# Eight projection units opened side by side in a two-block transformer kernel

## The reference, cut to what matters

```python
cs = jax.nn.silu(c)
mod = cs @ ada_w[i] + ada_b[i]              # c: 1 x 1024, ada_w[i]: 1024 x 3072, for i = 0, 1
shift, scale, gate = jnp.split(mod, 3, axis=-1)
h = x * (1.0 + scale) + shift               # x: 256 x 1024
q, k, v, z = jnp.split(h @ moba_w_in, 4)    # moba_w_in: 1024 x 4096; attention on q, k, v, gated by z
```

## Time and profile before

| | us |
|---|---|
| three runs, median (lowest, highest) | 838.95 (838.51, 839.56) |
| the profiled execution | 838.93 |
| its span, first to last instruction | 837.1 |
| busy: PE, DVE, ACT | 818.4, 615.7, 487.6 |
| unit 4 begins on PE (end of the opening) | 40.45 |
| unit 12 begins | 63.48 |
| unit 20 begins | 86.88 |
| mean DMA rate, 3 to 40 us, 44 to 78 us | 420 GB/s, 390 GB/s |

### The profile page before, as it was taken

One profiled execution on the slowest core, in us unless ns is written; L12 is line 12 of the kernel. 1 busy time (PEld: TensorE's weight loads), 2 busy tenths in 40 slices (PEclk: granted clock), 3 DMA queues, 4 the chain that ended last, 5 costly groups with the idle time before them and its releaser, 6 DMA issues.

```text
span 837.1 us, 17642 instructions
## 1 busy us (share of the span) xinstructions
PE 818.4 (98%) x6596; PEld 764.3 (91%) x6596; DVE 615.7 (74%) x1053; ACT 487.6 (58%) x901; POOL 68.2 (8%) x72
## 2 busy tenths in 40 slices
PE   6999999999999999999999999999999999999997
PEld 3899988999999998989898888999999999999885
DVE  4497876768989766977877779664777996888543
ACT  3444575567689754594665457566556554555444
POOL 1000002400001002214100011000002120000000
PEclk9999999999999999999999999999999999999999
DMA  9999963904552221435643426433455454544531
GB/s 374 388 364 391 369 251 143 350 5 151 168 186 99 102 103 52 156 146 191 213 158 144 152 82 221 152 133 142 180 177 201 167 186 155 197 172 179 201 101 50
DMA packets 22012, 153.85 MB, mean 184 GB/s; under 512 B 2496, under 2 KB 2752, under 8 KB 3904
## 3 DMA queue, kind: packets, MB, share of 16 engines
q1 hardware_dynamic: 20592, 145.69, 47.7%
q0 software_dynamic: 1360, 7.34, 2.3%
HBM read 151.97 MB, written 1.05 MB: 183 GB/s over the span
## 4 chain that ended last, share of the span: by engine, by line
PE 87%; DVE 6%; DMA 3%; ACT 3%; issue 1%; SPq 0%; DVEq 0%
PE ps L402 46%; PE ps L1276 7%; PE ps L505 7%; PE ps L475 4%; PE ps L436 2%; PE ps L445 1%; PE ps L467 1%; DVE w_lo L1969 1%; PE ps L842 1%; DMA raw<-in_moba_first 1%; DMA proj<-in_ada_first 1%; PE ps L579 1%; ACT w_hi L1316 1%; PE ps L602 1%; DMA memkv<-in_ada_first 1%
## 5 line engine op out<-in xcount | busy, mean ns | idle before, releaser
L1969 DVE TENSOR_TENSOR w_lo<-raw,w_hi 128x1024 fp32r<-128x1024 f32 x230 | 285.8, 1248 | 94.6 <-ACT w_hi L1316 93.3
L1316 ACT CAST w_hi<-raw 128x1024 fp32r<-128x1024 f32 (+1 forms) x230 | 239.8, 1050 | 164.8 <-PE ps L402 63.1
L402 PE MATMUL ps<-in_hi,w_hi 128*128 128x256 f32 x1120 | 160.8, 286 | 0.1
L402 PE MATMUL ps<-in_lo,w_hi 128*128 128x256 f32 x1120 | 157.2, 283 | 0.0
L402 PE MATMUL ps<-in_hi,w_lo 128*128 128x256 f32 x1120 | 157.1, 283 | 0.0
L402 PEld LDWEIGHTS ps<-in_hi,w_hi 128*128 128x128 f32 x1120 | 144.3, 191 | 4.5 <-issue 3.3
L402 PEld LDWEIGHTS ps<-in_hi,w_lo 128*128 128x128 f32 x1120 | 144.5, 192 | 0.0
L402 PEld LDWEIGHTS ps<-in_lo,w_hi 128*128 128x128 f32 x1120 | 144.3, 192 | 0.0
L2234 DVE SCALAR_TENSOR_TENSOR proj<-work,params,proj 128x256 f32 (+1 forms) x72 | 35.7, 496 | 8.0 <-ACT proj L1536 1.9
L2046 DVE SCALAR_TENSOR_TENSOR work<-raw,cs,work 128x1024 f32 x24 | 30.8, 1285 | 4.8 <-DVE w_lo L1969 1.6
L1276 PE MATMUL ps<-w_hi,in_hi 128*128 128x512 f32 x88 | 34.2, 389 | 0.0
(11 more groups left out here) (444 smaller groups left out, 1363.3 us busy)
## 6 DMA issues: line engine op xcount, KB each, us to landing
raw<-in_mixed SPq DMA_DIRECT2D x24, 1024.0 KB, 7.0
raw<-in_ffn_up SPq DMA_DIRECT2D x22, 1024.0 KB, 4.8
raw<-in_gdn_in SPq DMA_DIRECT2D x16, 1024.0 KB, 4.8
raw<-in_w_in SPq DMA_DIRECT2D x16, 1024.0 KB, 4.8
raw<-in_merge SPq DMA_DIRECT2D x12, 1024.0 KB, 4.8
raw<-in_ffn_down SPq DMA_DIRECT2D x11, 1024.0 KB, 4.7
raw<-in_branch SPq DMA_DIRECT2D x6, 1024.0 KB, 4.7
raw<-in_moba_out SPq DMA_DIRECT2D x4, 1024.0 KB, 6.7
```

The costliest lines, as they stand in the source:

```text
L402: mm = pe.matmul(half(u if bank is None else bank, 0), w[:, u, k * P:(k + 1) * P], a[:, base + k, :], start=(n == 0 and k == 0), stop=(n = ...
L1316: act.copy(w_hi[:, u, :], src).then_inc(hi_done, 1)
L1969: dve.tensor_tensor(w_lo[:, u, :], src, w_hi[:, u, :].bitcast(F32), ALU.subtract).then_inc(lo_done, 1)
```

## The change

The first eight units are now computed side by side, one feature tile after the other. Their weights come as rows: row k holds feature tile k of all eight units (0.5 MB), two rows to a ring slot, the first slot in two transfers, so that row 0 lands alone. `start_row(k, units)` runs the products of row k, first for units 0 and 4 (which share accumulator bank 0), then, behind `ada_columns`, for the other six; the low and high parts of a row are made by ACT and DVE between the operations of the opening. x comes in three transfers (tiles 0-1, 2-3, 4-7) instead of one. `WARM` goes from 11 idle products to 2, and the two idle products behind the second block go. The modulation blocks have semaphores of their own and no longer count as ring slots. The remaining modulation pieces no longer alternate one to one from the start: twelve ring places hold units 8 to 11 and pieces 0 to 7 (`opened`), then 16 units and 16 pieces alternate. The constants are issued after the eighth transfer of the loop instead of the twelfth; both are behind the fourteenth `mixed` transfer.

The core of the diff:

```diff
-WARM = 11
+WARM = 2
...
-ADA_FIRST = GROUP
-MIXED = ADA_FIRST + 16
-PLAIN = MIXED + 2 * 24
+ROWS = 8
+OPENED = (8, 10, 14, 16)
+MIXED = 20
+PLAIN = MIXED + 2 * 16
...
@@ SP @@
         load_ada(0)
-        for g in range(2):
-            sp.dma_start(raw[:, g, :], io["moba_first"][g]).then_inc(sem(f"slot_in{g}"), 16)
-        sp.dma_start(x_t[:], io["x_t"]).then_inc(sem("x_in"), 16)
+        sp.dma_start(raw[:, 0, 0:half_rows], io["moba_first"][0][:, 0:half_rows]).then_inc(sem("first_row_in"), 16)
+        sp.dma_start(x_t[:, 0:2, :], io["x_t"][:, 0:2, :]).then_inc(sem("x_in"), 16)
         load_ada(1)
-        for g in range(2):
-            landed(g)
-        for p in range(2, KT):
-            load_ada(p)
-            landed(p)
-        for c in range(2):
-            load_free(10 + c, io["mixed"][c])
-            landed(8 + c)
-        for start, stop in ((0, 3), (3, 5)):
+        sp.dma_start(raw[:, 0, half_rows:], io["moba_first"][0][:, half_rows:]).then_inc(sem("slot_in0"), 16)
+        load_ada(2)
+        sp.dma_start(x_t[:, 2:4, :], io["x_t"][:, 2:4, :]).then_inc(sem("x_mid_in"), 16)
+        load_rows(1)
+        load_ada(3)
+        landed(0)
+        load_ada(4)
+        load_rows(2)
+        sp.dma_start(x_t[:, 4:KT, :], io["x_t"][:, 4:KT, :]).then_inc(sem("x_rest_in"), 16)
+        landed(1)
+        load_ada(5)
+        load_ada(6)
+        load_rows(3)
+        load_ada(7)
+        for c in range(6):
+            load(4 + c, io["mixed"][c])
+        for start, stop in ((0, 2), (2, 4)):
...
@@ PE @@
+        def start_row(k, units):
+
+            pe.wait_ge(lo_done, place("moba_in", k) + 1)
             pe.wait_ge(*after("in0_hi", k + 1))
...
-        ada_products(1)
-        warm(2)
-        ada_columns(1)
-        ada_products(2)
-        pe.wait_ge(lo_done, 3)
-        start_tile(0)
-        ada_columns(2)
-        for p in range(3, KT):
-            ada_products(p)
-            start_tile(p - 2)
-            ada_columns(p)
-        start_tile(KT - 2)
-        start_tile(KT - 1)
-        pe.wait_ge(lo_done, 4)
-        unit(3)
-        project("moba_in", None, first_group=1, groups=5)
+        bank_pairs = [(u, u + GROUP) for u in range(GROUP)]
+        for k in range(KT - 1):
+            ada_products(k + 1)
+            start_row(k, bank_pairs[0])
+            ada_columns(k + 1)
+            start_row(k, [u for two in bank_pairs[1:] for u in two]).then_inc(unit_done, 1)
+        for two in bank_pairs:
+            start_row(KT - 1, two).then_inc(sem("first_banks"), 1)
+        pe.sem_inc(unit_done, 1)
+        for n in range(ROWS, 12):
+            pe.wait_ge(lo_done, place("moba_in", n) + 1)
+            pe.wait_ge(taken, GROUP + 2 * (n - ROWS + 1))
+            unit(n % GROUP)
+        project("moba_in", None, first_group=3, groups=3)
...
@@ ACT @@
+        highs_ahead = {0: (1,), 3: (4,)}
+        highs_behind = {1: (2, 3), 3: (5,), 5: (6, 7), 6: (8,)}
+        for k in range(KT - 1):
+            copy_rows(k + 1)
+            for n in highs_ahead.get(k, ()):
+                high("moba_in", n)
+            first_input(k + 1)
+            for n in highs_behind.get(k, ()):
+                high("moba_in", n)
+        for u in range(GROUP):
+            act.wait_ge(sem("first_banks"), u + 1)
+            for n in (u, u + GROUP):
+                act.copy(proj[:, n, :], half(u, n // GROUP)).then_inc(taken, 1)
+            if u == 1:
+                high("moba_in", 9)
+        for n in (10, 11):
+            high("moba_in", n)
+        project("moba_in", plain(proj), first_group=2, groups=4)
...
@@ DVE @@
+        lows_ahead = {0: (0,), 4: (4,)}
+        lows_behind = {1: (1,), 2: (2, 3), 4: (5,), 6: (6, 7), 7: (8,)}
...
+        rest(0, 9)
+        low("moba_in", 9)
+        for k, r in ((1, 11), (2, 12), (3, 13)):
+            rest(k, r)
+        low("moba_in", 10)
+        rest(4, 15)
+        low("moba_in", 11)
+        for k, r in ((5, 17), (6, 18), (7, 19)):
+            rest(k, r)
+        with dve.Fori(0, 4) as i:
```

More of the change, by code:

```diff
@@ L79, in place @@
 def place(name, n):
-    if name == "moba_in" and n < GROUP:
+    if name == "moba_in" and n < ROWS:
         return n
+    if name == "moba_in" and n < 12:
+        return OPENED[n - ROWS]
     if name == "moba_in" and n >= 28:
@@ L148, in _program @@
                 at += n
+    later = {"down_done": "ada_rows", "final_sq": "ada_copied", "final_gained": "ada_columns",
+             "final_sum": "mod_tile", "final_scale": "h0"}
+    for name, first in later.items():
+        shared[name], start[name] = first, KT
     sems = {}
@@ L369, in _ @@
         for c in range(2):
-            load(32 + c, io["mixed"][22 + c])
-        for c in range(2):
-            load(34 + c, io["moba_last"][c])
+            load(26 + c, io["moba_last"][c])
         for name, units in STAGES[1:]:
@@ L675, in ada_columns, with first_out @@
             mm.then_inc(sem("ada_columns"), 1)
-        def start_tile(k):
-            last = k == KT - 1
+        def first_out(u):
+            return half(u % GROUP, u // GROUP)
+        def start_row(k, units):
+            pe.wait_ge(lo_done, place("moba_in", k) + 1)
             pe.wait_ge(*after("in0_hi", k + 1))
-            for u in range(3):
-                pe.matmul(half(u, 0), w_hi[:, u, k * P:(k + 1) * P], in_hi[:, k, :], start=(k == 0), stop=False)
-                pe.matmul(half(u, 0), w_lo[:, u, k * P:(k + 1) * P], in_hi[:, k, :], start=False, stop=False)
+            slot = k % GROUP
+            for u in units:
+                pe.matmul(first_out(u), w_hi[:, slot, u * P:(u + 1) * P], in_hi[:, k, :],
+                          start=(k == 0 and u < GROUP), stop=False)
+                pe.matmul(first_out(u), w_lo[:, slot, u * P:(u + 1) * P], in_hi[:, k, :], start=False, stop=False)
             pe.wait_ge(*after("in0_lo", k + 1))
[L685 to L688, removed]
+            for u in units:
+                mm = pe.matmul(first_out(u), w_hi[:, slot, u * P:(u + 1) * P], in_lo[:, k, :],
+                               start=False, stop=(k == KT - 1 and u >= GROUP))
+            return mm
         pe.wait_ge(sem("cs_wide"), 1)
@@ L1379, in copy_rows, with first_input @@
             act.copy(ada_rows[k % 2], half(4 + k % 2, 0)).then_inc(sem("ada_copied"), 1)
[L1381 to L1386, removed]
+        def first_input(k):
             act.wait_ge(*after("h0", k + 1))
@@ L2008, in _ @@
         dve.memset(rows[:], 0.0)
-        for n in range(GROUP):
-            low("moba_in", n)
         flat_mod = mod[:].rearrange("p a b -> p (a b)")
@@ L2029, in _ @@
             dve.wait_ge(sem("mod_tile"), k + 1)
-            if k == 0:
-                dve.wait_ge(*after("x_in", 16))
+            if k in x_parts:
+                dve.wait_ge(*after(x_parts[k], 16))
             dve.tensor_scalar(first_h[:, k, :], x_t[:, k, :], mod[:, 0, 8 + k:9 + k], mod[:, 0, k:k + 1], ALU.mult, ALU.add
                               ).then_inc(sem("h0"), 1)
+            for n in lows_ahead.get(k, ()):
+                low("moba_in", n)
             dve.wait_ge(*after("in0_hi", k + 1))
```

74 lines of the change are left out of this document (42 added, 32 removed).

## The result

| | before | after |
|---|---|---|
| median of 8 runs each, us | 839.2 (838.46 to 840.26) | 843.02 (841.17 to 844.43) |
| ratio, 95% interval | | 1.0042 [1.0032, 1.0052] |
| profiled execution, us (span) | 838.93 (837.1) | 843.13 (841.0) |
| unit 8 begins on PE, us | 51.96 | 50.45 |
| unit 12 | 63.48 | 65.75 |

The account below looks back on a forecast made before the run. PE was taken to bound the kernel, with ring and DVE a parallel chain: 4.8 us won at unit 8, 3.3 lost to DVE's queue, 0.9 left at unit 20. 838.93 - 0.9 = 838.0 us; range 836.2 to 840.6.

Parts of the forecast that it names:

- the 2.5 us that it had allowed itself: Unit 20 on PE: the prediction called itself wrong altogether if it started more than 2.5 us away from 86.
- Block 1 at 11.2: Opening: the second modulation block lands at 10.6, idle products end at 11.2, then its products start at the low clock.
- I take it that the clock is up by then: Opening, row 0 at about 13.15: PE already runs at 2.4 GHz, with products 0.12 us apart.
- Rival 2: Opening: 2.4 GHz comes T later than 12.7 us, each us costing 0.5; chance 0.12 for T under 5, 0.09 above.
- Unit 8 at 47.2: End of the opening on PE: unit 8 begins at 47.2 instead of 51.96, 4.8 us earlier.
- the two waits before rows 2 and 6: Opening on PE: two waits of about 0.3 us each, for the chain from columns to low parts.
- rival 3: Opening: the two waits of the lows are a full operation each, 2.4 for 0.6 us, net +0.9; chance 0.09.
- Unit 12 at 14.8 us behind unit 8: Behind the opening: PE waits 3.3 us in all for DVE's eight rests and five lows; unit 12 at 62.0.
- Wait of about 1 us at unit 20: PE at unit 20, first behind the constants: its transfer holds PE about 1 us more, leaving 0.9 us gained.
- The ring's own part: Fifth mixed transfer issued at 47.1, landed 4.9 us later; fifth to fifteenth takes 31.6 us, to 83.6; unit 20 at 86.0.
- rival 1: Transfers behind the opening: the ring keeps pace, PE has no wait at unit 20; -1.9 to -2.4 us, some 836.8; chance 0.28.
- The hole in the DMA share near 48 us: Sign: the gap in the transfers, before at 40 to 44 us, moves to about 48 us, DMA share under 0.5.

Follow-up runs that it names:

- before, with two idle products: The kernel before with two idle products instead of eleven ahead of block 1, nothing else changed: median 842.33 us, ratio to before 1.0035.
- narrow rests: The changed kernel with rests 0 to 7 on 32 of their 1024 columns, most of the gate sum left out: median 838.97 us, ratio to before 1.0005.
- Waits filled: The changed kernel with two idle products ahead of unit 10 and five ahead of unit 12: median 840.91 us, ratio to before 1.0026.
- rests last: The changed kernel with units 8 to 27 each sharing a transfer with one modulation piece, the last four pieces in two own transfers: 838.76 us, ratio to before 0.9998.
- first slot whole: The changed kernel with the first ring slot in one transfer of 1 MB instead of two halves: median 844.99 us, ratio to before 1.0057.
- five idle products: The changed kernel with five idle products instead of two ahead of block 1: median 843.32 us, ratio to before 1.0047.

## Why the prediction was wrong, point by point

The mechanism of the ring and of DVE's queue was seen; the error is in the clock, twice, and in the first landing. At unit 20 the prediction had 86.0 and the trace has 90.37, 4.4 us too early and outside the 2.5 us that it had allowed itself:

- **Block 1 at 11.2** ("only 1.75 MB between: 6.28 + 4.3", and the idle products to 11.2): 12.35, and row 0 at 14.21 instead of 13.15, so +1.1. The rate of 2.46 us per MB itself was right for 1 MB blocks ("before, with two idle products" waits for block 1 to 16.13), but it didn't hold for the first half row and the first x piece (0.75 MB in 3.8 us). The size of this term was off.
- **"I take it that the clock is up by then, since PE does the same kinds of work up to 12.7":** this is the step that failed. The rate changed near 18.6: row 0 took 5.5 us (14.21 to 19.71) where row 1 took 3.5 (20.71 to 24.21), so +2.0. The kinds of work were the same up to 12.7 but their amount was not: nine idle products were gone, and PE stood 0.9 us for block 1. "Before, with two idle products" shows that this alone can cost 0.5 to 5 us. How much it costs is in part luck: in three other executions with this opening unit 8 came 1.4 to 1.5 us earlier. Rival 2 had this place, with T = 5.9, to which it gave 841.0 and 0.09 for all T above 5; its price of 0.5 per us counts from 12.7, though the forecast had block 1's products at the low rate anyway. The argument against it, that PE has more to do behind 12.7, says nothing of what comes before.
- **Unit 8 at 47.2:** 50.45, which is the two terms above and 0.2 for the two waits before rows 2 and 6 (0.40 each, 0.3 predicted; rival 3 falls). Still 1.5 us earlier than before.
- **Unit 12 at 14.8 us behind unit 8:** measured 15.3, so +0.5. The waits were 1.05 and 2.33 (3.3 in all predicted, 3.38 measured), ended by DVE's lows, and each moved PE by 0.15 more than its own length. From low 9 to low 12 DVE took 13.56 us (50.84 to 64.40), 13.3 predicted. This step was right in place and size; "narrow rests" shows its cause by taking the rests away, and finds 0.8 us there that the ring would have taken anyway.
- **Not in the forecast at all:** a wait of 2.33 us lets the clock fall, and unit 12 takes 4.46 us, +1.6. "Waits filled" shows that it is the wait. The price of a wait was counted as its length, and this one cost two thirds of its length again.
- **Wait of about 1 us at unit 20:** none, since everything on PE was later; -1.0. The ring's own part came out: the fifth mixed transfer was issued at 50.53 instead of 47.1, when low 8 and rest 0 were done, landed 4.9 us later, and the cast of unit 20 began at 87.01, 31.6 us behind that, as predicted. Its low ended at 89.3, 1.06 us ahead of PE. Where the opening is faster the wait is there: in "narrow rests" the cast began at 83.37 (83.6 predicted) and PE waited 1.08 us. So "no wait at unit 20" was no sign of rival 1 (the ring keeps pace) here, and "narrow rests" speaks against it.
- **The hole in the DMA share near 48 us:** found in two parts, from 44 to 46 (0.20; the fourth mixed transfer waits for rows 6 and 7 until 45.26) and from 50 to 52 (0.53; the fifth, until 50.53).

1.1 + 2.0 + 0.2 + 0.5 + 1.6 - 1.0 = 4.4, the whole difference at unit 20. The other 0.7 us of the miss came behind unit 20 (0.4) or outside the span (0.3), and their cause is open. Against the kernel before, the same trace reads: unit 8 -1.5, DVE's queue with the ring +3.8 (15.30 for 11.52), the fallen clock +1.6, behind it -0.4: +3.5 at unit 20. The clock's late rise is in the -1.5, which would have been -3.5 without it. In the prediction DVE's queue took 3.3 of a gain of 4.8; the gain was 1.5 and the queue took 3.8. Even the fastest run of the changed kernel (841.17) is 3.2 us above the forecast, so the draw of the clock's rise does not explain the miss by itself.

Open: why the first small pieces are slow; how much of the medians' differences the late rise of the clock makes in runs without a profile, which no figure on record shows; and the half rate at 303 us in one execution.

## What to carry to other kernels

Idle products ahead of the first real work can pay as long as the data aren't there: taking nine away cost the kernel before 3.3 us. Where the data come early they stand in the way instead: eleven of them cost "rests last" 4.1 us. Before cutting or adding them, look at which rate the products behind them run, and price the first rows at the low rate as well. Moving work earlier on one engine is worth what the engine that feeds it can follow: add up that engine's whole queue first, as the eight rests and five lows here, and expect the gain to come back as a wait wherever the queue is moved to. A wait of PE has a second price if the clock falls behind it; here idle products in the wait cost nothing and took that price away.

## What the runs showed of the hardware

- The rise to 2.4 GHz, read from the durations, came near 12.7 us in the kernel before; at 14.4, 15.3, 15.4 and 18.6 in four executions with the changed kernel's opening (19.5 with the first slot whole); at 12.8 and 15.6 with five idle products there; and at 20, 25.7 and 29 in three executions of the kernel before with two idle products. The granted clock reads 1.00 in these stretches all the same: at the start only durations tell.
- The granted clock fell to 0.50 for about 3.4 us behind a wait of 2.33 us, in three kernels' profiles (after, five idle products, first slot whole), and not behind one of 1.05 in the same traces nor behind one of 1.87 in "rests last".
- A half row of 512 KB and an x piece of 256 KB at the head of the queue took 1.9 and 2.0 us behind what was ahead of them, against 1.3 and 0.7 for their like a few us later.
